# Two of the four-tile products of each modulated norm between dense stages, computed by GpSimd instead of VectorE

## The chip, the cores and the metric

The kernel runs on one core of one Trainium2 chip. The metric is the device time of one execution in microseconds; a kernel is given by the median of its runs. TensorE multiplies matrices, VectorE and ScalarE work on tiles, GpSimd has so far only issued transfers and cleared one buffer, SyncE issues the loads of the weights.

## The reference

One inference step of a two-layer decoder trunk, for a prompt of 256 tokens and a sample group of 8 sequences of 8 tokens, 320 tokens in all (T = 320), with D_MODEL = 2048 and D_FF = 8192, in fp32.

```python
def rmsnorm(x, g):
    xf = x.astype(jnp.float32)
    y = xf * lax.rsqrt(jnp.mean(xf * xf, axis=-1, keepdims=True) + RMS_EPS)
    return (y * g.astype(jnp.float32)).astype(x.dtype)

def ada_modulate(c, w, b):
    m = jax.nn.silu(c) @ w + b
    shift, scale, gate = jnp.split(m[:, None, :], 3, axis=-1)
    return shift, scale, gate

def modulated_norm(x, g, shift, scale):
    return rmsnorm(x, g) * (1.0 + scale) + shift

def sq_relu_mlp(h, w1, w2):
    return jnp.square(jax.nn.relu(h @ w1)) @ w2
...
    for layer in range(DEPTH):
        shift, scale, gate = ada_modulate(c, W["ada_mix_w"][layer], W["ada_mix_b"][layer])
        h = modulated_norm(x, W["norm_mix"][layer], shift, scale)
        # layer 0: differential attention and RG-LRU mixer, layer 1: gated short convolution
        ...
        x = x + gate * y
        shift, scale, gate = ada_modulate(c, W["ada_mlp_w"][layer], W["ada_mlp_b"][layer])
        h = modulated_norm(x, W["norm_mlp"][layer], shift, scale)
        x = x + gate * sq_relu_mlp(h, W["mlp_w1"][layer], W["mlp_w2"][layer])
```

There are four modulated norms, numbered n = 0 to 3 in the kernel: before the mixer and before the MLP of each layer.

## The kernel before

**Data.** The activations lie transposed: `xT` is 16 tiles, each of 128 features on the partitions by 320 tokens. All products are fp32, made of three passes with halves of fewer bits: `h_hi` (the rounded value) and `h_lo` (what is left), the weights likewise `w_hi` and `w_lo`; TensorE adds hi x hi, lo x hi and hi x lo in one PSUM bank. The weights stream from HBM in chunks of 4 tiles by 256 columns into a ring of 4 slots: SyncE loads `raw`, ScalarE makes `w_hi` (L604), VectorE makes `w_lo` (L982), TensorE uses it (L1672, the helper of all matmuls).

**A dense stage** runs over pairs of output tiles; each pair takes four chunks, 16 input tiles. In its first pair TensorE waits for `h_ready` (h_inputs, L1784): for tile 0, tile 1, tiles 2 and 3, tiles 4 to 7, 8 to 11 and 12 to 15 in turn.

**A modulated norm** between two dense stages works in six units of 1, 1, 2, 4, 4, 4 tiles (UNITS, L360; u = 0 to 5). The sum of squares of the last pair is made by VectorE (L1133), TensorE sums it over the partitions, ScalarE computes the inverse root `rstd` with a logarithm and an exponential (L697, L699). Then for each unit:

- VectorE multiplies the tiles of `xT` by `rstd` into the buffer `tmp4` (scaled, L1058, the instruction of L1063), which counts `h_scaled`;
- ScalarE applies gain and shift to the 256 prompt tokens, one instruction for each tile (prompt, L707);
- VectorE applies them to the 64 sample tokens in two instructions (value, L1079 and L1082);
- ScalarE copies the result to `h_hi` (high, L715), VectorE subtracts it for `h_lo` (low_half, L1089), which counts `h_ready`.

`tmp4` has two halves of four tiles: tiles 0 to 3 and 8 to 11 use the first, 4 to 7 and 12 to 15 the second. Unit 4 and unit 5 wait until the half is free (L1062). The order on each engine is written out by hand; VectorE's is in norm (L1108): the product of a unit, its sample tokens, then `h_lo` of the unit before, and after `h_lo` of unit 3 one `w_lo` chunk. So the sample tokens of unit 5 stand ahead of `h_lo` of unit 4. ScalarE's is in norm (L725). The engines meet only by semaphores, and each does its own instructions in order.

The norm n = 0 has another order (norm_block), with the products spread among other work; n = 1, 2, 3 use norm. GpSimd issues the transfers of the cache pages, stores results, and clears `wgate` (L528).

Of the kernel before, what the change touches and what calls it, by code (L numbers as in the profile page):

```python
# [9 lines left out]
ALU = mybir.AluOpType  # L10
# [3 lines left out]
P = 128  # L14
# [4 lines left out]
T = SEQ + TS  # L19
# [119 lines left out]
def trunk_kernel(nc, A, O):  # L139
    with ExitStack() as ctx:  # L140
# [145 lines left out]
        def sems(text):  # L286
# [23 lines left out]
        sp_val, sp_fn = sems("sp_val sp_fn")  # L310
        ada_copied, fold_done, ada_turned, mod_ready = sems("ada_copied fold_done ada_turned mod_ready")
        x_ready = sems("x_ready")
        sq_ready, sq_summed, norm_log, norm_root, h_scaled, h_prompt, h_val, h_hi_ready, h_ready = sems(
            "sq_ready sq_summed norm_log norm_root h_scaled h_prompt h_val h_hi_ready h_ready")
        u_val, u_hi_ready, u_ready = sems("u_val u_hi_ready u_ready")
# [41 lines left out]
        GAIN = [ROW["norm_mix"], ROW["norm_mlp"], ROW["norm_mix"] + KT, ROW["norm_mlp"] + KT]  # L357
        MOD_READY = [8, 15, 21, 21]
        H_READY = [0, 10, 16, 22]
        UNITS = [(0, 1), (1, 1), (2, 2), (4, 4), (8, 4), (12, 4)]  # L360
        X_READY = [1, 9, 41, 49, 81]
        OPENING = [0, 4, 1, 5, 2, 6, 3, 7, 8, 9]
        BURSTS = [2, 2, 1, 1, 1, 1, 0, 0]

        @block.sync
        def _(sp):
# [151 lines left out]
        def _(pool):  # L518
            stores = [0]

            def store(dst, src):
                pool.dma_start(dst, src).then_inc(stored, 16)
                stores[0] += 1
# [43 lines left out]
            for b in range(NB):  # L567
                if b + 1 < NB:
                    keys(b + 1)
                values(b)  # L570

            pool.wait_ge(l_row, 1)
            store(O["cl_p"], lrow[0:3, :])
            store(O["cl_s"], lrow[3:27, :])
            store(O["h_p"], lrow[27:28, :])
            store(O["h_s"], lrow[28:36, :])
            pool.wait_ge(st_row, 1)
            store(O["sc_p"], srow_out[0:2, :])
            store(O["sc_s"], srow_out[2:18, :])
            yp = O["y_p"].rearrange("(a p) f -> a p f", p=P)  # L580
            for tt in range(3):
                pool.wait_ge(y_even, 2 * (tt + 1))
# [9 lines left out]
        def _(act):  # L592
# [108 lines left out]
            def prompt(n, u):  # L701

                first, count = UNITS[u]
                act.wait_ge(h_scaled, 6 * n + u + 1)
                for k in range(first, first + count):
                    out = tmp4[:, k // 4 % 2, k % 4, 0:SEQ]
                    ins = fn(out, out, ACT.Identity, scale=amp[:, k, 0:1], bias=mod[:, n, k, 0:1])  # L707
                ins.then_inc(h_prompt, 1)
# [254 lines left out]
        def _(dve):  # L963
# [109 lines left out]
            def value(n, u):  # L1073

                first, count = UNITS[u]
                out, tiles = tmp4[:, first // 4 % 2, first % 4:first % 4 + count], slice(first, first + count)
                dve.wait_ge(h_scaled, 6 * n + u + 1)
                sample = out[:, :, SEQ:T].rearrange("p t (b q) -> p t b q", b=NB)
                step(v.tensor_tensor(sample, sample, amp[:, tiles, 1:NC].unsqueeze(3).broadcast_to([P, count, NB, DS]),  # L1079
                                     ALU.mult))  # L1080
                settle()
                v.tensor_tensor(sample, sample, mod[:, n, tiles, 1:NC].unsqueeze(3).broadcast_to([P, count, NB, DS]),  # L1082
                                ALU.add).then_inc(h_val, 1)
# [24 lines left out]
            def norm():  # L1108

                n = N[0]  # L1110
                inverse_root()
                if n == 3:
                    dve.wait_ge(stored, 160)
                scaled(0)
                dve.wait_ge(amp_ready, n + 4)
                value(n, 0)
                for u in range(1, 6):
                    scaled(u)
                    value(n, u)
                    low_half(n, u - 1)  # L1120
                    if u == 4:
                        split(1)
                low_half(n, 5)
                N[0] += 1
# [1064 lines left out]
```

## Time and profile before

| | |
|---|---|
| median of 3 runs | 3152.55 us (3146.82 to 3153.94) |
| the profiled execution, its own time | 3152.81 us |
| its span in the trace | 3151.1 us |
| granted TensorE clock, mean | 0.983 of full speed |
| PE busy | 3056.1 us (97%) |
| VectorE (DVE) busy | 1480.9 us (47%) |
| ScalarE (ACT) busy | 1084.4 us (34%) |
| GpSimd (POOL) busy | 29.6 us (1%) |
| HBM read | 617.13 MB, 198 GB/s over the span |

An engine's busy share is an average over all stages; what a stretch is worth is read from the waits inside it. Line numbers such as L1063 are those of the kernel before. Times in an order of time count from the start of the span; "idle before" names the event that ended the idling. In this table and in the rows PE is TensorE, PEld its weight load, DVE VectorE, ACT ScalarE, POOL GpSimd.

### The profile page before, as it was taken

To read this page: it belongs to the slowest core of one execution; us is meant where nothing else is said; L and a number is where in the kernel's file an instruction comes from. 1 tells how busy PE (TensorE), PEld (TensorE's weight loads), DVE (VectorE), ACT (ScalarE), POOL (GpSimd) and SP (SyncE) were. 2 spreads that over 40 slices of the span, in tenths; PEclk is the share of its full clock that TensorE was granted. 3 is DMA by queue.
4 is the path that set the end of the run, shared out by engine and by line. 5 is a ranking of instruction groups with operands and counts; after the bars stand their busy time and mean duration, and the time that the engine had idled before them with its cause. 6 is when DMAs were issued, how large, how long until landed. Compare 5 with 4: busy or idle time off the path is not lost.

```text
span 3151.1 us, 53269 instructions
## 1 busy us (share of the span) xinstructions
PE 3056.1 (97%) x21011; PEld 2809.6 (89%) x21011; DVE 1480.9 (47%) x2057; ACT 1084.4 (34%) x1309; POOL 29.6 (1%) x55
## 2 busy tenths in 40 slices
PE   8999997899999999999999899999999999999998
PEld 4888853598899899889889899999899999999998
DVE  3556555455344344344345554445544444444443
ACT  3334443334322332332333433333433332332332
POOL 0000001000000000000000000000000000000000
PEclk8999998999999999999999999999999999999999
DMA  9986789545765765765774344444344444444543
GB/s 317 338 284 225 259 346 417 206 155 194 256 199 196 258 218 182 253 235 160 261 253 147 121 149 150 142 153 150 124 148 151 143 152 147 142 152 141 152 149 107
DMA packets 451959, 624.90 MB, mean 198 GB/s; under 512 B 16960, under 2 KB 402753, under 8 KB 433028
## 3 DMA queue, kind: packets, MB, share of 16 engines
q1 hardware_dynamic: 443776, 595.65, 57.1%
q0 software_dynamic: 6112, 22.84, 1.9%
q10 hardware_dynamic: 1926, 4.24, 0.4%
q8 instruction: 119, 1.95, 0.3%
q14 instruction: 26, 0.21, 0.0%
HBM read 617.13 MB, written 5.54 MB: 198 GB/s over the span
## 4 chain that ended last, share of the span: by engine, by line
PE 92%; DMA 4%; DVE 2%; issue 1%; ACT 1%; SPq 0%; POOL 0%; POOLq 0%; DVEq 0%; ACTq 0%
PE mm L1672 86%; PE aux L1672 5%; PE mm L1825 1%; DMA wide_first<-in_ada_mix_w 1%; DMA narrow<-in_ada_mlp_w 1%; DMA kpage<-in_cache_k 1%; DVE tmp L1063 1%; DMA vpage<-in_cache_v 1%; DMA second_row<-in_ada_mlp_w 0%; DVE h_lo L1089 0%; PE aux L2043 0%; DVE tmp L1079 0%; DVE tmp L1082 0%; DVE w_lo L982 0%; PE aux L1825 0%
## 5 line engine op out<-in xcount | busy, mean ns | idle before, releaser
L982 DVE TENSOR_TENSOR w_lo<-raw,w_hi 128x1024 fp32r<-128x1024 f32 x752 | 919.6, 1225 | 1325.9 <-ACT w_hi L604 1324.3
L604 ACT ACTIVATE w_hi<-raw 128x1024 fp32r<-128x1024 f32 x752 | 794.8, 1058 | 1703.9 <-PE mm L1672 1703.9
L1672 PE MATMUL mm<-h_hi,w_hi 128*128 128x320 f32 x3712 | 1167.6, 315 | 32.3 <-DVE h_lo L1089 18.9
L1672 PE MATMUL mm<-h_hi,w_lo 128*128 128x320 f32 x3712 | 1152.8, 311 | 0.0
L1672 PE MATMUL mm<-h_lo,w_hi 128*128 128x320 f32 x3712 | 1152.6, 311 | 0.0
L1672 PEld LDWEIGHTS mm<-h_hi,w_hi 128*128 128x128 f32 x3712 | 701.9, 189 | 132.8 <-issue 104.6
L1672 PE MATMUL mm<-u_hi,w_hi 128*128 128x320 f32 x2304 | 713.7, 310 | 0.0
L1672 PE MATMUL mm<-u_hi,w_lo 128*128 128x320 f32 x2304 | 712.0, 309 | 0.0
L1672 PE MATMUL mm<-u_lo,w_hi 128*128 128x320 f32 x2304 | 711.9, 309 | 0.0
L1672 PEld LDWEIGHTS mm<-h_lo,w_hi 128*128 128x128 f32 x3712 | 702.6, 189 | 0.2 <-issue 0.2
L1672 PEld LDWEIGHTS mm<-h_hi,w_lo 128*128 128x128 f32 x3712 | 702.2, 189 | 0.0
L1672 PEld LDWEIGHTS mm<-u_hi,w_hi 128*128 128x128 f32 x2304 | 432.5, 188 | 13.4 <-issue 13.4
L1672 PEld LDWEIGHTS mm<-u_lo,w_hi 128*128 128x128 f32 x2304 | 432.5, 188 | 0.0
L1672 PEld LDWEIGHTS mm<-u_hi,w_lo 128*128 128x128 f32 x2304 | 432.5, 188 | 0.0
L1672 PE MATMUL aux<-narrow,cs 128*32 128x512 f32 x856 | 122.0, 609 | 2.2 <-DMA narrow<-in_ada_mlp_w 2.2
L1318 DVE TENSOR_TENSOR u_lo<-mtmp,u_hi 128x640 f32 x64 | 52.8, 826 | 67.0 <-ACT u_hi L746 67.0
L746 ACT ACTIVATE u_hi<-mtmp 128x640 f32 x64 | 47.3, 739 | 98.5 <-DVE mtmp L1315 98.5
L1253 DVE SCALAR_TENSOR_TENSOR xT<-mm,mod,xT 128x256 f32 (+1 forms) x160 | 69.4, 476 | 0.0
L1315 DVE TENSOR_TENSOR mtmp<-mtmp 128x640 f32<-128x640 f32 x64 | 52.5, 820 | 0.0
L1672 PE MATMUL aux<-wide_first,cs 128*32 128x512 f32 x232 | 45.1, 679 | 5.8 <-DMA wide_first<-in_ada_mix_w 4.9
L744 ACT ACTIVATE mtmp<-mm 128x640 f32<-128x640 f32 x64 | 43.9, 686 | 0.0
L707 ACT ACTIVATE tmp<-tmp,mod,amp 128x256 f32<-128x256 f32 x64 | 34.0, 590 | 23.0 <-DVE amp L1070 14.6
(280 smaller groups left out, 1071.5 us busy)
## 6 DMA issues: line engine op xcount, KB each, us to landing
raw<-in_mlp_w SPq DMA_DIRECT2D x512, 512.0 KB, 3.7
narrow<-in_ada_mlp_w SPq DMA_DIRECT2D x70, 1024.0 KB, 5.0
raw<-in_w_in_odd SPq DMA_DIRECT2D x96, 512.0 KB, 3.8
narrow<-in_ada_mix_w SPq DMA_DIRECT2D x42, 1024.0 KB, 5.1
raw<-in_w_in_even SPq DMA_DIRECT2D x80, 512.0 KB, 6.9
wide_first<-in_ada_mix_w SPq DMA_DIRECT2D x58, 512.0 KB, 9.0
wide_later<-in_ada_mlp_w SPq DMA_DIRECT2D x20, 1024.0 KB, 14.3
raw<-in_w_out_even SPq DMA_DIRECT2D x32, 512.0 KB, 3.5
```

The source lines that it names most:

```text
L604: fn(w_hi[:, slot], raw[:, slot], ACT.Copy).then_inc(hi_ready, 1)
L707: ins = fn(out, out, ACT.Identity, scale=amp[:, k, 0:1], bias=mod[:, n, k, 0:1])
L744: fn(mtmp[:, r], mm[:, r, :, 0:T], ACT.Relu).then_inc(relu_out, 1)
L746: fn(u_hi[:, bass.ds(j, 2), :], mtmp[:, r], ACT.Copy).then_inc(u_hi_ready, 1)
L982: v.tensor_tensor(w_lo[:, slot], raw[:, slot], w_hi[:, slot].bitcast(F32), ALU.subtract).then_inc(lo_ready, 1)
L1063: v.tensor_tensor(tmp4[:, first // 4 % 2, first % 4:first % 4 + count], xT[:, first:first + count, :], rstd[:, :].unsqueeze(1).broadcast_t ...
L1253: ins = v.scalar_tensor_tensor(x, mm[:, r, m, 0:SEQ], g, x, ALU.mult, ALU.add)
L1315: v.tensor_tensor(mtmp[:, r], mtmp[:, r], mtmp[:, r], ALU.mult).then_inc(u_val, 1)
L1318: v.tensor_tensor(u_lo[:, bass.ds(j, 2), :], mtmp[:, r], u_hi[:, bass.ds(j, 2), :].bitcast(F32), ALU.subtract).then_inc(u_ready, 1)
L1672: return nc.tensor.matmul(out, lhsT, rhs, start=first, stop=last)
L1825: return nc.tensor.transpose(out, in_, const[0:rows, 0:rows])
```

## The change

In the norms n = 1, 2 and 3, GpSimd makes the products of units 3 and 5 (tiles 4 to 7 and 12 to 15) with the inverse root, into the same half of `tmp4`, and counts a new semaphore, `far_scaled`. Unit 3 waits for the inverse root; unit 5 also for `h_lo` of unit 3. VectorE leaves the two out of its order, and it and ScalarE wait for `far_scaled` where they waited for `h_scaled`. The norm n = 0 stays as it was. In GpSimd's own order the products of n = 1 and 2 stand after the stores of the recurrent state, those of n = 3 after the stores of the short convolution's state.

```diff
--- before.py
+++ after.py
@@ -310,6 +310,7 @@
         sp_val, sp_fn = sems("sp_val sp_fn")
         ada_copied, fold_done, ada_turned, mod_ready = sems("ada_copied fold_done ada_turned mod_ready")
         x_ready = sems("x_ready")
+        far_scaled = sems("far_scaled")
         sq_ready, sq_summed, norm_log, norm_root, h_scaled, h_prompt, h_val, h_hi_ready, h_ready = sems(
             "sq_ready sq_summed norm_log norm_root h_scaled h_prompt h_val h_hi_ready h_ready")
         u_val, u_hi_ready, u_ready = sems("u_val u_hi_ready u_ready")
@@ -357,10 +358,19 @@
         GAIN = [ROW["norm_mix"], ROW["norm_mlp"], ROW["norm_mix"] + KT, ROW["norm_mlp"] + KT]
         MOD_READY = [8, 15, 21, 21]
         H_READY = [0, 10, 16, 22]
+        SCALED = [1, 2, 3, 1, 4, 2]
         UNITS = [(0, 1), (1, 1), (2, 2), (4, 4), (8, 4), (12, 4)]
         X_READY = [1, 9, 41, 49, 81]
         OPENING = [0, 4, 1, 5, 2, 6, 3, 7, 8, 9]
         BURSTS = [2, 2, 1, 1, 1, 1, 0, 0]
+
+        def scaled_done(n, u):
+
+            if n == 0:
+                return h_scaled, u + 1
+            if u in (3, 5):
+                return far_scaled, 2 * (n - 1) + SCALED[u]
+            return h_scaled, 6 + 4 * (n - 1) + SCALED[u]
 
         @block.sync
         def _(sp):
@@ -569,14 +579,28 @@
                     keys(b + 1)
                 values(b)
 
+            def far_tiles(n):
+
+                for u in (3, 5):
+                    first, count = UNITS[u]
+                    pool.wait_ge(norm_root, n + 1)
+                    if u == 5:
+                        pool.wait_ge(h_ready, H_READY[n] + 4)
+                    nc.gpsimd.tensor_tensor(tmp4[:, 1, :, :], xT[:, first:first + count, :],
+                                            rstd[:, :].unsqueeze(1).broadcast_to([P, count, T]), ALU.mult
+                                            ).then_inc(far_scaled, 1)
+
             pool.wait_ge(l_row, 1)
             store(O["cl_p"], lrow[0:3, :])
             store(O["cl_s"], lrow[3:27, :])
             store(O["h_p"], lrow[27:28, :])
             store(O["h_s"], lrow[28:36, :])
+            far_tiles(1)
+            far_tiles(2)
             pool.wait_ge(st_row, 1)
             store(O["sc_p"], srow_out[0:2, :])
             store(O["sc_s"], srow_out[2:18, :])
+            far_tiles(3)
             yp = O["y_p"].rearrange("(a p) f -> a p f", p=P)
             for tt in range(3):
                 pool.wait_ge(y_even, 2 * (tt + 1))
@@ -701,7 +725,7 @@
             def prompt(n, u):
 
                 first, count = UNITS[u]
-                act.wait_ge(h_scaled, 6 * n + u + 1)
+                act.wait_ge(*scaled_done(n, u))
                 for k in range(first, first + count):
                     out = tmp4[:, k // 4 % 2, k % 4, 0:SEQ]
                     ins = fn(out, out, ACT.Identity, scale=amp[:, k, 0:1], bias=mod[:, n, k, 0:1])
@@ -1074,7 +1098,7 @@
 
                 first, count = UNITS[u]
                 out, tiles = tmp4[:, first // 4 % 2, first % 4:first % 4 + count], slice(first, first + count)
-                dve.wait_ge(h_scaled, 6 * n + u + 1)
+                dve.wait_ge(*scaled_done(n, u))
                 sample = out[:, :, SEQ:T].rearrange("p t (b q) -> p t b q", b=NB)
                 step(v.tensor_tensor(sample, sample, amp[:, tiles, 1:NC].unsqueeze(3).broadcast_to([P, count, NB, DS]),
                                      ALU.mult))
@@ -1115,7 +1139,8 @@
                 dve.wait_ge(amp_ready, n + 4)
                 value(n, 0)
                 for u in range(1, 6):
-                    scaled(u)
+                    if u not in (3, 5):
+                        scaled(u)
                     value(n, u)
                     low_half(n, u - 1)
                     if u == 4:
```

The order on VectorE in the norm n = 1, from the product of tiles 2 and 3 (128x640) on, before; `tmp_86` is `tmp4`, `h_lo` the low half, L1079 and L1082 the sample tokens:

```order
L1063 TENSOR_TENSOR tmp_86<-xT,rstd 128x640
L1079 TENSOR_TENSOR tmp_86<-tmp_86,amp 128x2x64
L1082 TENSOR_TENSOR tmp_86<-tmp_86,mod 128x2x64
L1089 TENSOR_TENSOR h_lo<-tmp_86,h_hi 128x320
L1063 TENSOR_TENSOR tmp_86<-xT,rstd 128x1280
L1079 TENSOR_TENSOR tmp_86<-tmp_86,amp 128x4x64
L1082 TENSOR_TENSOR tmp_86<-tmp_86,mod 128x4x64
L1089 TENSOR_TENSOR h_lo<-tmp_86,h_hi 128x640
L1063 TENSOR_TENSOR tmp_86<-xT,rstd 128x1280
```

And the same place of the changed kernel, whose lines L1087, L1103, L1106 and L1113 are those four:

```order
L1087 TENSOR_TENSOR tmp_86<-xT,rstd 128x640
L1103 TENSOR_TENSOR tmp_86<-tmp_86,amp 128x2x64
L1106 TENSOR_TENSOR tmp_86<-tmp_86,mod 128x2x64
L1113 TENSOR_TENSOR h_lo<-tmp_86,h_hi 128x320
L1103 TENSOR_TENSOR tmp_86<-tmp_86,amp 128x4x64
L1106 TENSOR_TENSOR tmp_86<-tmp_86,mod 128x4x64
L1113 TENSOR_TENSOR h_lo<-tmp_86,h_hi 128x640
L1087 TENSOR_TENSOR tmp_86<-xT,rstd 128x1280
```

The product of tiles 4 to 7 is gone from VectorE; the sample tokens of these tiles now follow the low half of tile 1 at once. At the end of the same norm, VectorE before, from the low half of tiles 4 to 7 on (L982 is a `w_lo` chunk):

```order
L1089 TENSOR_TENSOR h_lo<-tmp_86,h_hi 128x1280
L982 TENSOR_TENSOR w_lo<-raw,w_hi 128x1024
L1063 TENSOR_TENSOR tmp_86<-xT,rstd 128x1280
L1079 TENSOR_TENSOR tmp_86<-tmp_86,amp 128x4x64
L1082 TENSOR_TENSOR tmp_86<-tmp_86,mod 128x4x64
L1089 TENSOR_TENSOR h_lo<-tmp_86,h_hi 128x1280 x2
```

And of the changed kernel, where L1006 is the `w_lo` chunk:

```order
L1113 TENSOR_TENSOR h_lo<-tmp_86,h_hi 128x1280
L1006 TENSOR_TENSOR w_lo<-raw,w_hi 128x1024
L1103 TENSOR_TENSOR tmp_86<-tmp_86,amp 128x4x64
L1106 TENSOR_TENSOR tmp_86<-tmp_86,mod 128x4x64
L1113 TENSOR_TENSOR h_lo<-tmp_86,h_hi 128x1280 x2
```

The product of tiles 12 to 15 is gone; the two low halves at the end (tiles 8 to 11, then 12 to 15) still stand behind the sample tokens of tiles 12 to 15. On GpSimd, from the stores of the recurrent state on, before:

```order
L522 DMA out_cl_p<-lrow 3x1024
L522 DMA out_cl_s<-lrow 24x1024
L522 DMA out_h_p<-lrow 16x1x64
L522 DMA out_h_s<-lrow 8x1024
L522 DMA out_sc_p<-srow_out 2x2048
L522 DMA out_sc_s<-srow_out 16x2048
```

And of the changed kernel (L532 is the store, L589 the new function, whose first instruction is one that the compiler puts ahead):

```order
L532 DMA out_cl_p<-lrow 3x1024
L532 DMA out_cl_s<-lrow 24x1024
L532 DMA out_h_p<-lrow 16x1x64
L532 DMA out_h_s<-lrow 8x1024
L589 ISA
L589 TENSOR_TENSOR tmp_86<-xT,rstd 128x1280 x4
L532 DMA out_sc_p<-srow_out 2x2048
L532 DMA out_sc_s<-srow_out 16x2048
L589 TENSOR_TENSOR tmp_86<-xT,rstd 128x1280 x2
```

Four products of n = 1 and 2 stand between the two groups of stores, two of n = 3 behind the second.

## Rows read from the trace of the kernel before

**Rows 1.** The page: span, busy time of each engine, its share, instructions.

```profile
span 3151.1 us, 53269 instructions
...
PE 3056.1 (97%) x21011; PEld 2809.6 (89%) x21011; DVE 1480.9 (47%) x2057; ACT 1084.4 (34%) x1309; POOL 29.6 (1%) x55
```

**Rows 2.** View of waits, TensorE: who for whom, us in total, times, longest.

```profile
PE mm L1672 <- DVE h_lo L1089: 18.9, 12, 3.6
```

**Rows 3.** Order of time, VectorE, n = 1: start, duration, instruction, idle before.

```profile
738.71 0.49 DVE L1063 TENSOR_TENSOR tmp<-xT,rstd 128x320 f32<-128x320 f32 x1 [2.50 <-ACT rstd L699]
...
742.43 0.48 DVE L1089 TENSOR_TENSOR h_lo<-tmp,h_hi 128x320 fp32r<-128x320 f32 x1
742.83 1.48 DVE L1063 TENSOR_TENSOR tmp<-xT,rstd 128x1280 f32<-128x1280 f32 x1
744.35 0.43 DVE L1079 TENSOR_TENSOR tmp<-tmp,amp 128x256 f32<-128x256 f32 x1
...
746.00 1.49 DVE L1063 TENSOR_TENSOR tmp<-xT,rstd 128x1280 f32<-128x1280 f32 x1
...
748.33 1.48 DVE L1089 TENSOR_TENSOR h_lo<-tmp,h_hi 128x1280 fp32r<-128x1280 f32 x1
749.74 1.22 DVE L982 TENSOR_TENSOR w_lo<-raw,w_hi 128x1024 fp32r<-128x1024 f32 x1
750.87 1.48 DVE L1063 TENSOR_TENSOR tmp<-xT,rstd 128x1280 f32<-128x1280 f32 x1
752.39 0.43 DVE L1079 TENSOR_TENSOR tmp<-tmp,amp 128x256 f32<-128x256 f32 x1
...
753.19 1.49 DVE L1089 TENSOR_TENSOR h_lo<-tmp,h_hi 128x1280 fp32r<-128x1280 f32 x1
755.86 1.49 DVE L1089 TENSOR_TENSOR h_lo<-tmp,h_hi 128x1280 fp32r<-128x1280 f32 x1 [1.18 <-ACT h_hi L715]
```

**Rows 4.** Order of time, ScalarE, n = 1.

```profile
743.07 0.74 ACT L715 ACTIVATE h_hi<-tmp 128x640 fp32r<-128x640 f32 x1
744.35 2.07 ACT L707 ACTIVATE tmp<-tmp,mod,amp 128x256 f32<-128x256 f32 x4 [0.54 <-DVE tmp L1063]
746.51 1.27 ACT L715 ACTIVATE h_hi<-tmp 128x1280 fp32r<-128x1280 f32 x1
```

**Rows 5.** Order of time, TensorE, n = 1.

```profile
741.26 0.38 PE L1672 MATMUL mm<-h_hi,w_hi 128*128 128x320 f32 x1 [2.65 <-DVE h_lo L1089]
...
753.64 1.06 PE L1672 MATMUL aux<-narrow,cs 128*32 128x512 f32 x8
754.83 0.38 PE L1672 MATMUL mm<-h_hi,w_hi 128*128 128x320 f32 x1
```

**Rows 6.** Order of time, TensorE, n = 2 and n = 3.

```profile
1757.60 0.38 PE L1672 MATMUL mm<-h_hi,w_hi 128*128 128x320 f32 x1 [1.92 <-DVE h_lo L1089]
...
1762.46 0.39 PE L1672 MATMUL mm<-h_hi,w_hi 128*128 128x320 f32 x1 [1.11 <-DVE h_lo L1089]
...
2228.75 0.38 PE L1672 MATMUL mm<-h_hi,w_hi 128*128 128x320 f32 x1 [1.11 <-DVE h_lo L1089]
```

**Rows 7.** The chain that ended last, from 1760 us: start, duration, what.

```profile
1762.46 12.55 PE mm L1672 x84
```

**Rows 8.** Order of time, GpSimd, and VectorE's instruction beside its memset.

```profile
200.76 1.80 POOL L528 MEMSET wgate<- 128x2048 f32 x1 [198.68 <-PE aux L1672]
...
652.65 0.53 POOL L522 DMA_DIRECT2D out_h_s<-lrow  x1
...
200.83 1.23 DVE L982 TENSOR_TENSOR w_lo<-raw,w_hi 128x1024 fp32r<-128x1024 f32 x1 [0.33 <-ACT w_hi L604]
```

**Rows 9.** View by stretches, n = 1: busy of each engine, granted clock (PEclk), DMA.

```profile
core 0: us, PE busy (x) PEld busy (x) DVE busy (x) ACT busy (x) POOL busy (x), PEclk, DMA share, GB/s
...
743.00:746.00 3.00, 1.93 (x6) 1.53 (x6) 2.90 (x4) 2.39 (x5) 0.00 (x0) 0.50 0.52 178
...
750.00:754.00 4.00, 4.00 (x28) 3.61 (x32) 3.93 (x5) 2.74 (x5) 0.00 (x0) 1.00 0.40 117
```

## The prediction, as put on record before the changed kernel ran

> **What bounds the kernel now.** I read the page first: TensorE is busy 97% of a 3151.1 us span, VectorE 47%, GpSimd 1% [rows 1]. So VectorE's work costs time only where TensorE waits for it. The view of waits says where that is: TensorE's matmuls waited 12 times, 18.9 us in all, for `h_lo` of L1089, the last step of a modulated norm [rows 2]. There are three such norms between dense stages (n = 1, 2, 3), which reach TensorE near 741, 1757 and 2229 us [rows 5, 6], each with four waits. Everything here happens in those three stretches of some 17 us; the first norm (n = 0) keeps its path.
>
> Then the order of time in one stretch, n = 1. VectorE runs almost without a gap from 738.71 (first product with the inverse root) until `h_lo` of tiles 8 to 11 is written, at 753.19 + 1.49 = 754.68 [rows 3]. ScalarE stands beside it: `h_hi` of tiles 2, 3, then four activations on tiles 4 to 7, then their `h_hi` [rows 4]. TensorE starts at 741.26 after 2.65 us of idling; at 753.64 it turns to the eight modulation matmuls, and goes on with tiles 8 to 11 at 754.83 [rows 5]. So in n = 1 the end of `h_lo` for tiles 8 to 11 (754.68) and the end of those eight (754.70) meet. In n = 2 TensorE waits 1.92 us for tiles 4 to 7 and 1.11 us for tiles 8 to 11; in n = 3 it waits 1.11 us for tiles 8 to 11 again [rows 6]. After that it never waits: 84 matmuls in 12.55 us without a break [rows 7], and `h_lo` of tiles 12 to 15 ends at 757.35 [rows 3], while 24 matmuls from 754.83 at 12.55 / 84 = 0.149 us each last until 758.4, so it has 1.0 us to spare. **The point that sets the end is therefore `h_lo` of tiles 8 to 11.** Each microsecond by which it moves goes into the span, three times.
>
> **What the change removes.** Two VectorE products per norm, 128x1280, tiles 4 to 7 (742.83, 1.48 us) and 12 to 15 (750.87, 1.48 us) [rows 3]; from start to the next start they hold VectorE 1.52 us each, of which 0.10 lies under the instruction before, so about 1.42 each comes off its chain. Six in all.
>
> **What it adds.** Six GpSimd products of the same size, and no DMA. The first of a norm may start with the inverse root, at 738.7; the second when `h_lo` of tiles 4 to 7 is written (748.33 + 1.48 = 749.81). Two waits are added on VectorE: the sample-token product of tiles 4 to 7 waits for the first, that of tiles 12 to 15 for the second. Behind the latter stands `h_lo` of tiles 8 to 11, the point that sets the end, so GpSimd's second product is on the path although tiles 12 to 15 are not due. GpSimd's queue is empty then: the last of the four small stores ahead of the first product went out at 652.65 [rows 8], and nothing is queued behind the products that anyone waits for.
>
> **How long a GpSimd product takes (P).** No row shows one. The nearest is its memset of 128x2048: 1.80 us, one stream, 0.88 ns for a column [rows 8]. One stream of 1280 columns is 1.13 us, the lower end; two inputs and an output, one after the other, are 3 x 1.13 = 3.38 us, the upper end. With the two inputs alone in series it is 2.25. I take the middle of the last two, 2.8 us, since some of the writing should lie beside the reading, and some of it not.
> The Trainium skill ("GPSIMD Engine Reference", Elementwise: side-by-side cycle accounting) gives 4497 ns for a fp32 tensor_tensor of 2048 columns; scaled to 1280 that is an estimate of 2.8 us, and the sum would be the same.
>
> **Do the two engines run side by side?** VectorE's work in these stretches is all tensor_tensor with both inputs in SBUF, and so is GpSimd's. The only overlap that the trace shows is the memset from 200.76 to 202.56 beside VectorE's 128x1024 subtraction, which took 1.23 us as everywhere [rows 8]; it says that a GpSimd instruction which only writes costs VectorE nothing, and nothing about one that reads. So both ends have to be worked out.
>
> Side by side (no cost of overlap). First part: GpSimd ends at 738.7 + 2.8 = 741.5, before VectorE asks at 742.9. VectorE's chain is 1.42 shorter, but ScalarE takes over as the limit: its activations on tiles 4 to 7 start at 743.81, when its `h_hi` of tiles 2, 3 is done, instead of 744.35, their `h_hi` ends 0.54 sooner, at 747.24 [rows 4], and `h_lo` of tiles 4 to 7 starts at 747.26 instead of 748.33: 1.07 gained. Second part, from the end of that `h_lo` to the end of the next: before 754.68 - 749.81 = 4.87 us. Now max(1.14 subtraction, P) + 0.80 (two small products, as 752.39 to 753.19) + 1.49 = 5.09: 0.22 lost. Together -0.8 a norm, -2.5 in three.
>
> One at a time (each GpSimd product holds up VectorE for its whole length, or the reverse). First part: VectorE's chain gets P = 2.8 in place of 1.42, +1.4; if the stall falls before `h_lo` of tiles 0 and 1, which is likely since both engines are released by the same event at 738.7, TensorE starts 2.8 us late and ScalarE's `h_hi` of tiles 2, 3 ends at 746.6, so `h_lo` of tiles 4 to 7 starts at 746.6 + 2.16 (activations) + 1.27 (`h_hi`) + 0.02 = 750.05, +1.7. Second part: 1.14 + 2.8 + 0.80 + 1.49 = 6.23 instead of 4.87, +1.4, whichever of the two goes first. Sum +3.1 a norm; with P = 2.25 it is +2.0, with 3.38 +4.3. Three norms: +9.3 (6 to 13).
>
> I take one at a time. VectorE has no other second operand in these stretches than one from SBUF, both engines are asked to read the same tile `xT` and the same `rstd` at the same moment, and in such a sum the cost falls on the same point wherever the stall lands; but rows alone leave this open.
> The Trainium skill ("SBUF — State Buffer", Who interferes with whom) states that a VectorE instruction with two SBUF inputs contends with a GpSimd instruction that reads SBUF, and not with one that only writes, and that the later one blocks until the first has finished. The memset row agrees with its second half; no row shows the first. By that rule the sum is the one-at-a-time sum, +9.3; without it, -2.5. This sentence, and no row, is why one at a time stands first below.
>
> **Sum.** Profiled execution 3152.81 us (span 3151.1 and 1.7 around it) + 9.3 = 3162.1; the median of the runs is 0.3 below it, so 3161.8.
>
> **The rivals.**
> - *Side by side*, the other sign: the move does what it says, 3152.5 - 2.5 = 3150. For it: the chain is really shorter, and the memset overlapped freely. Against it: even then GpSimd's P of 2.8 against 1.42 on the path eats the second half of the gain. The gain passes 0.2% only with P near 1.13: then the second part is 1.14 + 0.80 + 1.49 = 3.43, -1.4, and the three norms give -7.5, 3145. It decides from P + overlap cost below about 1.7 us.
> - *Shared reads*: VectorE's instructions stretch while GpSimd runs but do not stop; half way between the two ends, (9.3 - 2.5) / 2 = +3.4, 3156. Nothing for or against it in the rows.
> - *The clock stays low after the longer stop.* TensorE's granted clock was 0.50 (1.2 GHz) from 743 to 746, after the idling of 2.65 us and short bursts with gaps, and 1.00 (2.4 GHz) from 750 [rows 9]. That costs nothing now since it falls under VectorE's chain. One at a time, TensorE stops some 5.5 us before its first matmul and 1.11 + 1.4 = 2.5 before tiles 8 to 11. Should those 24 matmuls run at 1.2 GHz they take twice 3.6 us: +3.6, and three norms give 9.3 + 10.8 = +20, 3173. Against it: 1.92 us of waiting at 1757 was followed by full clock at 1762, where 84 matmuls took 0.149 each [rows 6, 7].
> - *A slow first product.* What GpSimd loads for it can be fetched in the 85 us after its last store [rows 8]; if not, the first product alone is longer, by as much as P again in my bounds, +2.8 once, 3165, still inside the first case's range. The Trainium skill ("GPSIMD Engine Reference", the part on dispatch) puts the first call of a freshly loaded routine at about 6 us; by that 3168.
>
> **How the numbers follow.** One at a time 0.50, side by side 0.27, shared reads 0.15, clock low 0.08. What a measurement of this kernel can tell from no change is 0.2%, 6.3 us. Slower by more: 0.44 of the first (P above 2.3) and all of the last, 0.52. Faster by more: 0.06, out of side by side with a short P. Within: 0.42. The likeliest case alone spans 3158 to 3165; the range has to take in side by side at 3150 with the runs' spread of some 2 us below it, and part of the clock case: 3148 to 3168.
>
> **What would show it.** Two GpSimd products a norm of 2.3 to 3.4 us; the first beginning within 0.6 us of the inverse root; VectorE idle, or one small product stretched by 2 to 3 us, before `h_lo` of tile 0; TensorE's longest wait for `h_lo` in n = 1 up from 2.65 to about 5.4; `h_lo` of tiles 4 to 7 about 1.7 and that of tiles 8 to 11 about 3.1 later than before, counted from the inverse root; waits for L1089's successor above 25 us in total. It is wrong if VectorE's small products keep 0.23 and 0.43 us while GpSimd runs: then side by side holds. If P is under 2 us, the size is wrong even if the mechanism holds.

## The result, and the profile after

The changed kernel takes 3161.92 us (median of 8 runs, 3158.68 to 3162.51), the kernel before 3151.22 us (median of 8, 3146.31 to 3153.94). The ratio is 1.0036, with a 95% interval of 1.0026 to 1.0045: slower by 8 to 14 us, clear of the 0.2% that was called no change. The forecast was 3161.8 in a range of 3148 to 3168, worked out as 9.3 us on top of 3152.5; the two medians here differ by 10.7. The profiled execution of the changed kernel took 3161.92 us with a span of 3160.3, against 3152.81 and 3151.1.

TensorE's waits for the low half, which were 18.9 us in 12 waits [rows 2], in the changed kernel (its L1113 is the old L1089; who waits for whom, us in total, times, longest):

```profile
PE mm L1697 <- DVE h_lo L1113: 28.3, 9, 6.1
```

The six new products on GpSimd, in order of time (start, duration, instruction, idle before with its end):

```profile
738.64 3.18 POOL L589 TENSOR_TENSOR tmp<-xT,rstd 128x1280 f32<-128x1280 f32 x1 [85.58 <-ACT rstd L723]
751.18 3.82 POOL L589 TENSOR_TENSOR tmp<-xT,rstd 128x1280 f32<-128x1280 f32 x1 [9.36 <-DVE h_lo L1113]
1749.05 3.19 POOL L589 TENSOR_TENSOR tmp<-xT,rstd 128x1280 f32<-128x1280 f32 x1 [994.05 <-ACT rstd L723]
1761.60 3.81 POOL L589 TENSOR_TENSOR tmp<-xT,rstd 128x1280 f32<-128x1280 f32 x1 [9.36 <-DVE h_lo L1113]
...
2218.08 3.18 POOL L589 TENSOR_TENSOR tmp<-xT,rstd 128x1280 f32<-128x1280 f32 x1 [99.84 <-ACT rstd L723]
2230.63 3.81 POOL L589 TENSOR_TENSOR tmp<-xT,rstd 128x1280 f32<-128x1280 f32 x1 [9.36 <-DVE h_lo L1113]
```

They come in pairs: 3.18 us for tiles 4 to 7, 3.81 for tiles 12 to 15, the same in all three norms. What VectorE does in the norm n = 1 beside them (the lines of [rows 3], whose numbers are now L1087, L1103, L1106 and L1113):

```profile
738.59 0.49 DVE L1087 TENSOR_TENSOR tmp<-xT,rstd 128x320 f32<-128x320 f32 x1 [2.50 <-ACT rstd L723]
739.18 2.72 DVE L1103 TENSOR_TENSOR tmp<-tmp,amp 128x64 f32<-128x64 f32 x1
741.93 0.22 DVE L1106 TENSOR_TENSOR tmp<-tmp,mod 128x64 f32<-128x64 f32 x1
...
749.54 1.49 DVE L1113 TENSOR_TENSOR h_lo<-tmp,h_hi 128x1280 fp32r<-128x1280 f32 x1
750.95 1.22 DVE L1006 TENSOR_TENSOR w_lo<-raw,w_hi 128x1024 fp32r<-128x1024 f32 x1
755.03 0.43 DVE L1103 TENSOR_TENSOR tmp<-tmp,amp 128x256 f32<-128x256 f32 x1 [2.86 <-POOL tmp L589]
...
755.83 1.49 DVE L1113 TENSOR_TENSOR h_lo<-tmp,h_hi 128x1280 fp32r<-128x1280 f32 x1
758.50 1.49 DVE L1113 TENSOR_TENSOR h_lo<-tmp,h_hi 128x1280 fp32r<-128x1280 f32 x1 [1.18 <-ACT h_hi L739]
```

The second row shows the price of GpSimd's first product. It is the first product for the sample tokens, 128x64, which takes 0.23 us in the kernel before. Here it takes 2.72 and ends at 741.90, 0.08 us after GpSimd's product (738.64 + 3.18 = 741.82). At the other end of the norm VectorE's weight chunk (750.95 to 752.17) was under way when GpSimd's second product was released, and it keeps its 1.22 us; this time GpSimd's row is the long one, 3.82, and VectorE then stands until 755.03. ScalarE's part, for [rows 4]:

```profile
745.44 0.74 ACT L739 ACTIVATE h_hi<-tmp 128x640 fp32r<-128x640 f32 x1
746.08 2.06 ACT L731 ACTIVATE tmp<-tmp,mod,amp 128x256 f32<-128x256 f32 x4
748.24 1.27 ACT L739 ACTIVATE h_hi<-tmp 128x1280 fp32r<-128x1280 f32 x1
```

And TensorE's, for [rows 5] (start, duration, instruction, its wait):

```profile
743.63 0.61 PE L1697 MATMUL mm<-h_hi,w_hi 128*128 128x320 f32 x1 [5.14 <-DVE h_lo L1113]
...
751.18 0.38 PE L1697 MATMUL mm<-h_hi,w_hi 128*128 128x320 f32 x1 [1.20 <-DVE h_lo L1113]
...
757.47 0.38 PE L1697 MATMUL mm<-h_hi,w_hi 128*128 128x320 f32 x1 [1.54 <-DVE h_lo L1113]
```

TensorE starts 5.04 us after VectorE's first product (743.63 against 738.59), before 2.55, and reaches tiles 8 to 11 after 18.88, before 16.12 [rows 3, 5]. This last distance, from VectorE's first product of a norm to TensorE's first matmul on tiles 8 to 11, is called M below. It is what the argument of the prediction rests on, and it agrees to 0.03 us between the norms of the kernel before and of the changed kernel, while the runs of one kernel spread over 4 us and more.

| M, us | n = 1 | n = 2 | n = 3 | median, us | ratio to before, 95% interval |
|---|---|---|---|---|---|
| before | 16.12 | 16.09 | 16.12 | 3151.22 | |
| changed | 18.88 | 18.87 | 18.86 | 3161.92 | 1.0036 (1.0026 to 1.0045) |
| u3_alone | 17.45 | 17.44 | 17.45 | 3154.94 | 1.0014 (1.0004 to 1.0023) |
| u5_alone | 17.52 | 17.53 | 17.51 | 3156.86 | 1.0015 (1.0006 to 1.0025) |
| first_late | 19.18 | 19.13 | 19.15 | 3162.25 | 1.0035 (1.0024 to 1.0046) |
| both_split_moved | 18.03 | 18.02 | 18.01 | 3158.91 | 1.0021 (1.0010 to 1.0032) |
| write_only | 14.77 | 13.70 | 13.71 | 3148.87 | one run |
| one_input | 15.64 | 15.53 | 15.53 | 3146.94 | one run |
| psum_operand | 18.86 | 18.89 | 18.86 | 3166.57 | one run |
| split_moved | 16.90 | 15.12 | 15.08 | 3147.69 | 0.9993 (0.9984 to 1.0002) |
| reordered | 16.60 | 14.95 | 14.58 | 3145.93 | 0.9982 (0.9973 to 0.9992) |

The kernel before was run again beside each group of experiments, and the ratios are to those runs: a median of 3150.94 beside u3_alone, u5_alone, first_late and both_split_moved, 3150.42 beside split_moved and reordered, and one run of 3153.34 beside the three with one run.

**Where the 9.2 us of span come from.** M grew by 2.76, 2.78 and 2.74: 8.3 us. Between the norms nothing moved: from TensorE's tiles 8 to 11 in n = 1 to VectorE's first product in n = 2 it is 991.5 us in both (738.71 + 16.12 to 1746.37, and 738.59 + 18.88 to 1749.00), and 450.2 in both from n = 2 to n = 3. The last 1.0 us lies behind n = 3, and the view by stretches shows something there that costs time (PEclk, the third column from the right, is the granted clock):

```profile
core 0: us, PE busy (x) PEld busy (x) DVE busy (x) ACT busy (x) POOL busy (x), PEclk, DMA share, GB/s
...
2238.00:2240.00 2.00, 2.00 (x9) 2.00 (x9) 2.00 (x2) 1.79 (x2) 0.00 (x0) 0.50 0.00 0
...
2241.00:2243.00 2.00, 2.00 (x16) 2.00 (x15) 0.70 (x1) 0.78 (x1) 0.00 (x0) 1.00 0.42 100
```

TensorE ran at 0.50, its lower level of 1.2 GHz, for 3.4 us from 2237.3 on, right after it had waited 2.51 us for tiles 8 to 11; its matmuls on tiles 12 to 15 began 23.98 us after VectorE's first product, in n = 1 and 2 22.46. That is 1.5 us. But the whole stretch from tiles 8 to 11 of n = 3 to the end grew by only 1.05 us, and in the eleven kernels of the table, one profiled execution each, it lies anywhere between 919.3 and 923.4 us (before 922.35, changed 923.40), the highest being the changed kernel. So the 8.3 us are the change's; how much of the last 1.0 is, one pair of executions can't say. The medians differ by 2.4 us more than M, and that rest is open too.

### The profile page after: what moved, and what is told of

Read it like the earlier page. It is cut to its first block, busy times and chain, and to the rows that moved or that the text cites. A ratio compares the mean times of both kernels' runs of the same rounds, so it can differ in the third digit from the quotient of the medians.

```text
span 3160.3 us, 53274 instructions
## 1 busy us (share of the span) xinstructions
PE 3051.7 (97%) x21011; PEld 2810.0 (89%) x21011; DVE 1480.2 (47%) x2051; ACT 1084.7 (34%) x1309; POOL 50.7 (2%) x61
## 4 chain that ended last, share of the span: by engine, by line
PE 92%; DMA 4%; DVE 2%; ACT 1%; issue 1%; POOL 0%; SPq 0%; POOLq 0%; ACTq 0%; DVEq 0%
PE mm L1697 86%; PE aux L1697 5%; DMA kpage<-in_cache_k 1%; PE mm L1850 1%; DMA wide_first<-in_ada_mix_w 1%; DMA narrow<-in_ada_mlp_w 1%; DMA second_row<-in_ada_mlp_w 0%; POOL tmp L589 0%; DVE tmp L1103 0%; DVE h_lo L1113 0%; ACT tmp L731 0%; ACT h_hi L739 0%; PE aux L2068 0%; DVE tmp L1087 0%; DVE p_s L1503 0%
## 5 line engine op out<-in xcount | busy, mean ns | idle before, releaser
L1006 DVE TENSOR_TENSOR w_lo<-raw,w_hi 128x1024 fp32r<-128x1024 f32 x752 | 919.7, 1225 | 1327.0 <-ACT w_hi L628 1325.4
L1697 PE MATMUL mm<-h_hi,w_hi 128*128 128x320 f32 x3712 | 1169.5, 315 | 40.7 <-DVE h_lo L1113 28.3
L1697 PEld LDWEIGHTS mm<-u_hi,w_hi 128*128 128x128 f32 x2304 | 432.7, 188 | 13.4 <-issue 13.4
```

The source lines that it names most:

```text
L1006: v.tensor_tensor(w_lo[:, slot], raw[:, slot], w_hi[:, slot].bitcast(F32), ALU.subtract).then_inc(lo_ready, 1)
L1697: return nc.tensor.matmul(out, lhsT, rhs, start=first, stop=last)
```

## The experiments

### One product at a time

`u3_alone`: of the changed kernel's two, GpSimd makes only the product of tiles 4 to 7.

```diff
-                for u in (3, 5):
+                for u in (3,):
                     first, count = UNITS[u]
...
-                    if u not in (3, 5):
+                    if u not in (3,):
                         scaled(u)
```

> GpSimd makes only the product of tiles 4 to 7; VectorE makes that of tiles 12 to 15 again. M is the time from VectorE's first product of a norm to TensorE's first matmul on tiles 8 to 11: 16.1 us before, 18.9 in the changed kernel. One at a time: the first sample-token product stays stretched to 2.7 us, M = 16.1 + 1.3 = 17.4 in each norm, +4 us in three, 3155. Waits alone (the stretched row is not GpSimd's doing): M = 16.1 - 1.1 = 15.0, 3148.

VectorE's first sample-token product in n = 1:

```profile
740.43 2.72 DVE L1103 TENSOR_TENSOR tmp<-tmp,amp 128x64 f32<-128x64 f32 x1
```

M is 17.45, 17.44, 17.45, about 1.33 more each, to 0.05 as expected; the medians differ by 4.0 us. The "waits alone" theory wanted 15.0 and is out.

`u5_alone`: only the product of tiles 12 to 15 (the same edit with `(5,)`).

> GpSimd makes only the product of tiles 12 to 15. One at a time: the first sample-token product is back at 0.23 us and TensorE starts 2.55 us after VectorE's first product, as before; GpSimd's product is 3.8 us long beside the weight chunk's subtraction, M = 16.1 + 1.4 = 17.5, +4.3 us, 3155.5. If the 1.0 us by which this product exceeded the first part's were not a wait for VectorE but its own length, the same M; both_split_moved tells these apart. The two halves together should make the changed kernel: 4.0 + 4.3 = 8.3 of its 9.2 in span.

M is 17.52, +1.42 each. GpSimd's product, and VectorE's first two instructions, in n = 1 of this kernel:

```profile
748.40 3.80 POOL L589 TENSOR_TENSOR tmp<-xT,rstd 128x1280 f32<-128x1280 f32 x1 [96.78 <-DVE h_lo L1113]
```

```profile
737.15 0.49 DVE L1087 TENSOR_TENSOR tmp<-xT,rstd 128x320 f32<-128x320 f32 x1 [2.50 <-ACT rstd L723]
737.75 0.23 DVE L1103 TENSOR_TENSOR tmp<-tmp,amp 128x64 f32<-128x64 f32 x1
```

With no GpSimd product beside it the sample-token product takes its 0.23 us again; what was stretched in the changed kernel was stretched by GpSimd. The parts add up: 1.33 + 1.42 = 2.75 of 2.76. The medians differ by 5.9 us, where M gives 4.3 and 4.3 was expected. In one of its three norms (n = 2) TensorE ran at 1.2 GHz for 3.4 us again in its matmuls on tiles 8 to 11, after a wait of 2.34 us, and they took 1.5 us longer; the experiment was not made for this.

### Does it matter where the hold falls?

`first_late`: GpSimd's first product waits until VectorE is itself waiting for it.

```diff
                     pool.wait_ge(norm_root, n + 1)
+                    if u == 3:
+                        pool.wait_ge(h_ready, H_READY[n] + 2)
```

> As the changed kernel, but GpSimd's first product also waits for h_lo of tile 1, so it runs while VectorE has nothing to do but wait for it. One at a time with the price on tiles 4 to 7 and later: TensorE's first matmul is back at 2.55 us after VectorE's first product, no row is stretched, GpSimd's first product is 2.7 to 2.8 us (it no longer waits for VectorE), and M = 19.0, the same as in the changed kernel, 3161 to 3163. Rival, that the late start of TensorE (and its clock) is what costs: M under 17, 3154.

GpSimd's first product of n = 1, and TensorE's first and fifth wait:

```profile
744.91 2.90 POOL L591 TENSOR_TENSOR tmp<-xT,rstd 128x1280 f32<-128x1280 f32 x1 [89.88 <-DVE h_lo L1115]
```

```profile
743.12 0.38 PE L1699 MATMUL mm<-h_hi,w_hi 128*128 128x320 f32 x1 [2.65 <-DVE h_lo L1115]
...
759.74 0.38 PE L1699 MATMUL mm<-h_hi,w_hi 128*128 128x320 f32 x1 [1.14 <-DVE h_lo L1115]
```

VectorE's row at 741.16 is back at 0.23 us, TensorE starts at 743.12, 2.56 us after VectorE's first product (740.56), and yet M is 19.18, 0.3 more than in the changed kernel, and the time is the same, 3162.25. So the late start of TensorE was a symptom and not the price. Either the product holds VectorE at the start of the norm, or VectorE waits for it in the middle; the same point pays. The expected 19.0 was 0.15 to 0.2 too low; the product took 2.90 us and not 2.75, and began 0.16 after `h_lo` of tile 1 was written.

`both_split_moved`: nothing of VectorE's beside the second product.

```diff
                     low_half(n, u - 1)
-                    if u == 4:
-                        split(1)
+                split(1)
                 low_half(n, 5)
```

> As the changed kernel, but the weight chunk's subtraction stands after h_lo of tiles 8 to 11 instead of ahead of the sample tokens of tiles 12 to 15, so nothing of VectorE's lies beside GpSimd's second product. One at a time: that product is 2.7 to 2.8 us instead of 3.8, and the stretch from h_lo of tiles 4 to 7 to that of tiles 8 to 11 is 0.1 + 2.8 + 0.8 + 1.5 = 5.2 instead of 6.3: M = 17.8, 3 x 1.1 = 3.3 us less than the changed kernel, 3158. If 3.8 is the product's own length there: M = 18.9, no change.

```profile
739.79 3.18 POOL L589 TENSOR_TENSOR tmp<-xT,rstd 128x1280 f32<-128x1280 f32 x1 [85.57 <-ACT rstd L723]
752.33 2.97 POOL L589 TENSOR_TENSOR tmp<-xT,rstd 128x1280 f32<-128x1280 f32 x1 [9.36 <-DVE h_lo L1113]
```

```profile
750.70 1.49 DVE L1113 TENSOR_TENSOR h_lo<-tmp,h_hi 128x1280 fp32r<-128x1280 f32 x1
755.34 0.42 DVE L1103 TENSOR_TENSOR tmp<-tmp,amp 128x256 f32<-128x256 f32 x1 [3.15 <-POOL tmp L589]
```

The second product now takes 2.97 us instead of 3.82: 0.85 of its length in the changed kernel was waiting for VectorE's weight chunk. M is 18.03, 0.85 less than 18.88 (expected 1.1 less, with a product of 2.75). Here the other direction of the hold is shown: the engine that comes second waits, whichever it is. The first product, beside VectorE's 128x320, keeps its 3.18. And it is not a shared tile that the two engines quarrel over: the weight chunk (`w_lo` from `raw` and `w_hi`) touches nothing that GpSimd's product reads or writes, and holds it all the same.

### What in GpSimd's instruction holds VectorE

`write_only`: GpSimd fills the tiles instead of multiplying them.

```diff
-                    nc.gpsimd.tensor_tensor(tmp4[:, 1, :, :], xT[:, first:first + count, :],
-                                            rstd[:, :].unsqueeze(1).broadcast_to([P, count, T]), ALU.mult
-                                            ).then_inc(far_scaled, 1)
+                    nc.gpsimd.memset(tmp4[:, 1, :, :], 0.5).then_inc(far_scaled, 1)
```

> GpSimd fills the four tiles with a constant instead of multiplying them (it leaves the normalisation of tiles 4 to 7 and 12 to 15 out in n = 1 to 3); everything else, the waits too, is the changed kernel's. If GpSimd holds VectorE up only by reading SBUF: the first sample-token product is 0.23 us although GpSimd is busy beside it, GpSimd's instruction takes 1.1 us, M falls to 14 or less, 3147 or less. If any GpSimd instruction, or the new waits, hold VectorE up: the product is stretched to about 1 us.

GpSimd and VectorE at the start of n = 1:

```profile
742.14 1.16 POOL L589 MEMSET tmp<- 128x1280 f32 x1 [85.55 <-ACT rstd L721]
```

```profile
742.11 0.49 DVE L1085 TENSOR_TENSOR tmp<-xT,rstd 128x320 f32<-128x320 f32 x1 [2.50 <-ACT rstd L721]
742.70 0.23 DVE L1101 TENSOR_TENSOR tmp<-tmp,amp 128x64 f32<-128x64 f32 x1
```

VectorE's instruction at 742.70 lies wholly inside GpSimd's (742.14 to 743.30) and takes 0.23 us. None of VectorE's other rows in this norm is longer than before either. All of the changed kernel's waits are there, and nothing is held. M is 14.77, 13.70, 13.71, some 6 us less in three norms than before: this is about what the move would have been worth if the product were as short as a fill and cost VectorE nothing. In n = 1 the expected 14 was missed. TensorE came to the limit itself there: it was done with tiles 4 to 7 at 13.7 in all three norms, and in n = 1 its eight modulation matmuls stand next. The one run took 3148.87, where 3147 or less was expected and the kernel before took 3153.34.

`one_input`: GpSimd copies the four tiles (a `tensor_copy` of `xT` in the same place).

> GpSimd copies the four tiles instead of multiplying them (it leaves the inverse root out for tiles 4 to 7 and 12 to 15 in n = 1 to 3): one input read, one output. Its length shows how much of 2.8 us is the second input: 1.2 to 1.9 us expected. If reading is what holds VectorE up, the first sample-token product ends when the copy ends (stretched to 0.8 to 1.5 us); if only two-input instructions on both sides meet, it stays at 0.23 us.

```profile
737.60 1.57 POOL L589 COPY tmp<-xT 128x1280 f32<-128x1280 f32 x1 [85.57 <-ACT rstd L721]
```

```profile
738.16 1.08 DVE L1101 TENSOR_TENSOR tmp<-tmp,amp 128x64 f32<-128x64 f32 x1
```

One input read is enough: the 128x64 product is stretched to 1.08 us and ends at 739.24, 0.07 after the copy (739.17). The copy takes 1.57 us of which 0.45 lies beside VectorE's first product, so 1.1 once that is done, about as long as the fill. The multiply of the changed kernel takes 2.74 from the same moment (739.08 to 741.82). The second input and the multiplication add 1.6 us for 1280 columns; no run separates the two.

`psum_operand`: one more VectorE instruction in n = 3, with one operand from PSUM; its result is not used.

```diff
                 scaled(0)
+                if n == 3:
+                    v.tensor_tensor(ares[:, :], mm[:, 0, 0, :], ares[:, :], ALU.mult)
                 dve.wait_ge(amp_ready, n + 4)
```

> The changed kernel with one more VectorE instruction in n = 3, right after the first product: 128x512, one operand from PSUM and one from SBUF, its result used by nobody. Held up are only instructions with two SBUF inputs: it starts 0.5 us after the first product's start and takes 0.7 us beside GpSimd's product, the sample-token product behind it ends where it did (3.3 us after the first product's start) and M stays 18.9. Any VectorE work is held up: it is stretched to 3 us or more and M is 19.5.

GpSimd's first product of n = 3, and beside it VectorE's first product, the added instruction, and the sample-token product:

```profile
2224.28 3.19 POOL L589 TENSOR_TENSOR tmp<-xT,rstd 128x1280 f32<-128x1280 f32 x1 [99.84 <-ACT rstd L723]
```

```profile
2224.23 0.49 DVE L1087 TENSOR_TENSOR tmp<-xT,rstd 128x320 f32<-128x320 f32 x1 [2.50 <-ACT rstd L723]
2224.64 0.68 DVE L1140 TENSOR_TENSOR ares<-mm,ares 128x512 f32<-128x512 f32 x1
2225.24 2.31 DVE L1103 TENSOR_TENSOR tmp<-tmp,amp 128x64 f32<-128x64 f32 x1
```

The added instruction, 128x512, begins at 2224.64 in the middle of GpSimd's product and takes 0.68 us, on the line through 0.49 for 320 and 0.82 for 640 columns, so unhindered; the next, with two SBUF inputs and an eighth of its size, takes 2.31 and ends at 2227.55, 0.08 after GpSimd. Nor did GpSimd wait for the added instruction: its product takes 3.19, as in the changed kernel. M in n = 3 is 18.86, unchanged: the 0.68 us were free. So VectorE is not stopped as an engine; of the two instructions that began beside this product only the one with two inputs from SBUF was held. (This is one row in one norm, and an instruction with a single input from SBUF and none from PSUM was not tried. The time of this run, 3166.57, is high because VectorE's first product of n = 1 came at 743.5 instead of 738.6, ahead of anything changed, and because TensorE was at 1.2 GHz during its matmuls on tiles 8 to 11 in n = 2 and n = 3, which cost 1.3 and 1.5 us.)

### A version without GpSimd

The trace of before has VectorE idle 1.18 us ahead of the last low half [rows 3], and the weight chunk stands ahead of the point that sets the end. `split_moved` is the kernel before with that chunk moved (the edit of both_split_moved).

> The kernel before, all products on VectorE, with the weight chunk's subtraction moved behind h_lo of tiles 8 to 11, where VectorE idled 1.2 us. h_lo of tiles 8 to 11 ends 1.1 us earlier; in n = 1 TensorE is held by its own eight modulation matmuls, so M falls from 16.1 to 15.0 in n = 2 and 3 and to 16.0 in n = 1: -2.4 us, 3149 (ratio 0.9992). Rival: the weight ring is late (the chunk is ready 4 us later) and TensorE waits for it at tiles 12 to 15: no gain.

M falls in n = 2 and 3 by 1.0, as expected, but rises in n = 1 to 16.90. The view by stretches of n = 1 (in the kernel before, whose n = 1 begins 0.9 us later, PEclk was 0.50 from 747 to 749 and 0.98 from 749 to 751):

```profile
747.00:749.00 2.00, 1.68 (x7) 1.27 (x5) 1.93 (x4) 1.91 (x5) 0.00 (x0) 0.50 0.00 0
749.00:751.00 2.00, 1.95 (x7) 1.98 (x8) 1.93 (x3) 1.74 (x3) 0.00 (x0) 0.50 0.00 0
751.00:753.00 2.00, 2.00 (x14) 2.00 (x14) 2.00 (x3) 1.91 (x5) 0.00 (x0) 0.95 0.00 0
```

Up to TensorE's first matmul on tiles 4 to 7, 11.24 us after VectorE's first product, both kernels do the same. TensorE stayed at 1.2 GHz until 13.4 us after that product, in before until 10.4, and now that VectorE no longer is the limit the slow matmuls on tiles 4 to 7 are, with the eight modulation matmuls behind them. The time is 0.9993 of before (0.9984 to 1.0002), no difference shown. Of the expected 2.4 us, M gives 1.2.

`reordered`: all products on VectorE, and each low half as early as its `h_hi` allows.

```diff
-                for u in range(1, 6):
+                for u in range(1, 4):
                     scaled(u)
                     value(n, u)
                     low_half(n, u - 1)
-                    if u == 4:
-                        split(1)
+                scaled(4)
+                low_half(n, 3)
+                value(n, 4)
+                scaled(5)
+                low_half(n, 4)
+                value(n, 5)
+                split(1)
                 low_half(n, 5)
```

> The kernel before, all products on VectorE, in another order at the end of the norm: product of tiles 8 to 11, h_lo of 4 to 7, sample tokens of 8 to 11, product of 12 to 15, h_lo of 8 to 11, sample tokens of 12 to 15, weight chunk, h_lo of 12 to 15. h_lo of tiles 4 to 7 starts 0.5 us earlier (then ScalarE's h_hi holds it), h_lo of 8 to 11 2.0 us earlier, TensorE's own matmuls on tiles 4 to 7 then hold it: M = 15.4 in n = 1, 14.2 in n = 2 and 3: -4.4 us, 3147 (ratio 0.9986). Rival: with its waits gone from here TensorE waits at tiles 12 to 15 instead, gain under 2 us.

VectorE's products and low halves at the end of n = 1, and the stretches beside them:

```profile
741.35 1.49 DVE L1063 TENSOR_TENSOR tmp<-xT,rstd 128x1280 f32<-128x1280 f32 x1
743.16 1.49 DVE L1089 TENSOR_TENSOR h_lo<-tmp,h_hi 128x1280 fp32r<-128x1280 f32 x1 [0.32 <-ACT h_hi L715]
...
745.37 1.48 DVE L1063 TENSOR_TENSOR tmp<-xT,rstd 128x1280 f32<-128x1280 f32 x1
746.78 1.49 DVE L1089 TENSOR_TENSOR h_lo<-tmp,h_hi 128x1280 fp32r<-128x1280 f32 x1
...
750.41 1.49 DVE L1089 TENSOR_TENSOR h_lo<-tmp,h_hi 128x1280 fp32r<-128x1280 f32 x1 [0.20 <-ACT h_hi L715]
```

```profile
745.00:747.00 2.00, 2.00 (x8) 2.00 (x9) 1.98 (x3) 1.49 (x3) 0.00 (x0) 0.50 0.00 0
747.00:749.00 2.00, 2.00 (x15) 2.00 (x14) 1.97 (x4) 1.97 (x4) 0.00 (x0) 0.89 0.00 0
```

```profile
749.67 1.06 PE L1677 MATMUL aux<-narrow,cs 128*32 128x512 f32 x8
```

`h_lo` of tiles 8 to 11 ends at 748.27, 14.2 us after VectorE's first product (734.07), 1.8 earlier than before. TensorE does not come for it until 16.60: it was at 0.50 from 741 to 747, finished tiles 4 to 7 only near 749.6, and had its eight modulation matmuls to do. In n = 2 and 3 M is 14.95 and 14.58, expected 14.2. The ratio is 0.9982 (0.9973 to 0.9992): faster than before, by an amount (0.18%) that is just under the 0.2% called no change, and faster than the changed kernel by 16 us. M alone gives +0.5 - 1.1 - 1.5 = -2.2 us; the medians say -4.5, the ratio's interval -2.5 to -8.5. That the rest is the order's doing is not shown.

## Why the prediction was right

- **The point that sets the end.** It was to be `h_lo` of tiles 8 to 11, and each microsecond there was to go into the span three times. It did: 8.3 of 9.2 us are M, and the distances between the norms are equal to 0.1 us.
- **One at a time or side by side.** No row decided it; the forecast took the first with a chance of 0.50. It is shown now: the 128x64 product held for 2.72 us, GpSimd's product held for 0.85 by the weight chunk, no hold by a fill and none of an instruction with a PSUM operand. The Trainium skill ("SBUF — State Buffer", Who interferes with whom) was the only ground for preferring it, and these traces agree with each part of what was cited, 0.23 us beside a fill and 2.72 beside a multiply.
- **The length P.** Taken as 2.8 from bounds of 1.13 and 3.38. The rows are 2.90 (first_late) and 2.97 (both_split_moved) when nothing lies beside it; 2.74 is the part that follows VectorE's first product in the changed kernel. The estimate of 2.8 from the figure of the Trainium skill ("GPSIMD Engine Reference", Elementwise: side-by-side cycle accounting) is 0.1 to 0.2 below the two unhindered rows.
- **First part, +1.7 forecast, +1.33 measured.** This is the term that was mis-sized. The step counted the whole P as stall. GpSimd started 0.05 us after VectorE's first product and, as its 3.18 us against 2.90 to 2.97 alone suggest, did not get far until that was done, so the sample-token product was 2.49 us late and not 2.8; the other 0.06 lies in the steps from ScalarE's `h_hi` of tiles 2, 3 on and was not followed up. `h_lo` of tiles 4 to 7 began 10.95 us after the first product, before 9.62, forecast 11.3.
- **Second part, +1.4 forecast, +1.42 measured** (u5_alone alone; in the changed kernel from 751.03 to 757.32 = 6.29, forecast 6.23).
- **Sum.** 3 x 3.1 = 9.3 was forecast, and 3 x 2.76 = 8.3 came by the mechanism named. The measured change is larger than M makes it, 9.2 between the two spans and 10.7 between the medians. One thing is seen that adds to M, the rival that was given 0.08: the clock. Its trigger was right, the stop before tiles 8 to 11 grown to 2.5 us, and its place too. But it fell in one norm of three (n = 3; the stop of n = 2 was the same, 2.52, and the level stayed), and cost 1.5 us where 3.6 were worked out, since the low level ended after 3.4 us, before the 24 matmuls were through. Whether it makes up the rest is not shown, for the stretches ahead of n = 1 and behind n = 3 vary by several us from one execution to the next.
- **The closeness of 3161.8 to 3161.92 is luck.** The kernel before was taken at 3152.5, from three runs, and its eight runs gave 3151.22; the growth was taken at 9.3 and was 10.7. The two errors, of opposite sign, cancel.
- **Side by side** would have given M of 15.3 and **shared reads** 17.2; **slow first product**: GpSimd's first row, 3.18, is as long as the third and the fifth, so nothing was paid there.
- Of the signs listed, those on the mechanism all came: one small product stretched by 2.5 us ahead of `h_lo` of tile 0, TensorE's longest wait in n = 1 at 5.14 (forecast about 5.4), the waits in total 28.3 (above 25), the first GpSimd product 0.05 us behind VectorE's. Three sizes were off: `h_lo` of tiles 4 to 7 came 1.33 later and not 1.7, that of tiles 8 to 11 2.76 and not 3.1, and GpSimd's second product took 3.8 us, outside 2.3 to 3.4, because it stood 0.85 us for the weight chunk.

## What to carry to other kernels

Before moving an elementwise product from VectorE to GpSimd, ask what VectorE does meanwhile: if it is two-input work from SBUF, the move replaces d microseconds of VectorE (1.42 here) with P of GpSimd (2.7 to 3.0), and where VectorE's chain is the limit it grows by about P - d for each product, wherever the hold falls (1.33 and 1.42 us here, 1.6 in first_late). VectorE being idle is not enough: in first_late it was idle for all of P and the norm was longer still, because it was waiting for that very product. Of VectorE's instructions, the one here with an operand in PSUM ran freely beside GpSimd's product; the move may pay beside such work, which no run here tried. And where an engine's order is written by hand, look first for work that stands ahead of the critical item without being due: moving one weight chunk and two low halves gave 0.18% where the second engine cost 0.36%.

## What the runs showed of the hardware that was not expected

- Coming first kept VectorE its turn for one instruction only. VectorE, which had come first, did one 0.49 us instruction (to 739.08) and then stood for 2.5 us: GpSimd's product had been released at 738.64, and VectorE's next instruction came at 739.18. Whether the gap of 0.1 us between the two is what let GpSimd in was not tried.
- A held instruction's row is long rather than preceded by idle time. VectorE's busy time in the changed kernel, 1480.2 us, is nearly that of before (1480.9), although six products of 1.48 are gone: 8.9 us less work, three holds of 2.5 us shown as busy. In first_late, which has the same instructions and no stretched row, it is 1472.3. A busy share does not tell work from standing.
- The clock's low level after the stop at the beginning of a norm does not end at a fixed place. In n = 1 it lasted until 10.4 us after VectorE's first product in before and until 13.4 in split_moved, which had done the same up to there; in n = 2 of before it ended at about 6.2 (PEclk 0.71 from 1752 to 1753, 1.00 from 1753 on). As long as VectorE's chain is the limit this costs nothing; once the chain is shortened it can be what remains (n = 1 of split_moved and reordered).
